# Latent attention as expanded 64-row heads, and differential before forgetting attention in one pipeline

## The reference

```python
# layer 2, even_mixer
o_a = fox_attention(aq, ak, av, log_f)     # 8 heads of 64; scores + (c_q - c_k), c = cumsum(log_f)
o_b = diff_attention(q1, q2, k1, k2, bv, lam)  # 4 heads, values of width 128; p1 - lam * p2
o_b = rms_norm_2(o_b, subln) * (1.0 - lam_init)
# layer 3, odd_mixer
c_kv = rms_norm_2(ckv, kv_norm)            # one latent of width 128 for all heads
q_abs = jnp.einsum('bshn,rhn->bshr', q_nope, w_uk)
o_lat = dsa_attention(q_abs, q_rope, c_kv, k_rope, iq, iw, ik, top_k)
    # s = (q_abs . c_kv + q_rope . k_rope) * scale over the selected keys; o = softmax(s) @ c_kv
o_c = jnp.einsum('bshr,rhd->bshd', o_lat, w_uv)
o_d = stick_breaking_attention(sq, sk, sv)
```

## Time and profile before

| what | value |
| --- | --- |
| median of 3 runs | 1994.19 us (1992.67 to 1994.88) |
| the profiled execution's own time | 1992.21 us |
| its span in the trace | 1990.4 us |
| PE busy | 1874.2 us, 94% |
| DVE busy | 1102.0 us, 55% |
| ACT busy | 758.8 us, 38% |
| POOL busy | 112.8 us, 6% |
| granted TensorE clock, mean | 0.971 of full |

### The profile page before, as it was taken

How to read it: one execution, slowest core, us unless ns; L and a number is a source line. 1 busy time by engine, 2 the same in 40 slices (tenths; PEclk the granted TensorE clock), 3 DMA queues, 4 the chain that set the end, 5 groups by cost and what they waited for, 6 DMA issues and landing times.

```text
span 1990.4 us, 23667 instructions
## 1 busy us (share of the span) xinstructions
PE 1874.2 (94%) x8984; PEld 1493.0 (75%) x8984; DVE 1102.0 (55%) x1661; ACT 758.8 (38%) x1094; POOL 112.8 (6%) x114
## 2 busy tenths in 40 slices
PE   4996999999999998779999999999978899999998
PEld 2884688888887887458888888877845688888886
DVE  4789554444323454664767663256895256767422
ACT  4225543333324212663544532232265344444321
POOL 0000010000011002601000000000000010000000
PEclk8997999999999998889999999998989999999999
DMA  4330032323232422002222232331200023223231
GB/s 149 128 106 22 7 111 94 105 84 105 85 111 101 149 85 85 1 1 84 88 103 99 91 106 92 118 101 60 91 16 1 22 85 106 92 98 105 85 106 64
DMA packets 25720, 166.26 MB, mean 84 GB/s; under 512 B 3082, under 2 KB 3210, under 8 KB 6704
## 3 DMA queue, kind: packets, MB, share of 16 engines
q1 hardware_dynamic: 23904, 159.88, 23.1%
q0 software_dynamic: 1744, 5.37, 0.9%
HBM read 163.10 MB, written 2.13 MB: 83 GB/s over the span
## 4 chain that ended last, share of the span: by engine, by line
PE 87%; DVE 6%; ACT 2%; POOL 2%; issue 1%; DMA 0%; SPq 0%; DVEq 0%; ACTq 0%
PE ps L365 25%; PE ps L367 25%; PE ps L366 25%; POOL tmp L331 2%; PE ps L538 2%; PE ps L380 2%; PE ps L379 2%; PE ps L378 2%; DVE cacc L1254 1%; PE ps L519 1%; PE ps L502 1%; DVE ring L1307 1%; PE ps L493 1%; PE ps L411 1%; ACT ring L877 1%
## 5 line engine op out<-in xcount | busy, mean ns | idle before, releaser
L365 PE MATMUL ps<-a_hi,w_hi 128*128 128x512 f32 x1616 | 636.9, 394 | 21.6 <-DVE w_lo L1079 16.6
L366 PE MATMUL ps<-a_lo,w_hi 128*128 128x512 f32 x1616 | 631.7, 391 | 0.0
L367 PE MATMUL ps<-a_hi,w_lo 128*128 128x512 f32 x1616 | 631.7, 391 | 0.0
L365 PEld LDWEIGHTS ps<-a_hi,w_hi 128*128 128x128 f32 x1616 | 305.3, 189 | 91.5 <-DVE w_lo L1079 17.8
L366 PEld LDWEIGHTS ps<-a_lo,w_hi 128*128 128x128 f32 x1616 | 305.0, 189 | 65.4 <-issue 2.4
L367 PEld LDWEIGHTS ps<-a_hi,w_lo 128*128 128x128 f32 x1616 | 304.9, 189 | 64.2
L1079 DVE TENSOR_TENSOR w_lo<-raw,w_hi 128x2048 fp32r<-128x2048 f32 x82 | 192.2, 2345 | 243.6 <-ACT w_hi L732 243.6
L732 ACT CAST w_hi<-raw 128x2048 fp32r<-128x2048 f32 x82 | 156.1, 1904 | 416.3 <-PE ps L367 337.8
L365 PE MATMUL ps<-h_hi,w_hi 128*128 128x512 f32 x528 | 206.3, 391 | 0.0
L367 PE MATMUL ps<-h_hi,w_lo 128*128 128x512 f32 x528 | 205.5, 389 | 0.0
L366 PE MATMUL ps<-h_lo,w_hi 128*128 128x512 f32 x528 | 205.5, 389 | 0.0
(11 more groups left out here) (215 smaller groups left out, 2061.3 us busy)
## 6 DMA issues: line engine op xcount, KB each, us to landing
raw<-weights_dram SPq DMA_DIRECT2D x148, 1024.0 KB, 4.8
xT<-x_in_dram SPq DMA_DIRECT2D x8, 256.0 KB, 7.4
bias_t<-bias_rows_scratch POOLq DMA_DIRECT2D x8, 256.0 KB, 5.0
ncb<-decay_rows_scratch POOLq DMA_DIRECT2D x8, 256.0 KB, 4.5
out_dram<-xT SPq DMA_DIRECT2D x8, 256.0 KB, 2.0
vec<-vectors_dram SPq DMA_DIRECT2D x1, 282.5 KB, 2.9
ring<-ramp_dram POOLq DMA_DIRECT2D x1, 260.0 KB, 5.2
tmp<-positions_dram POOLq DMA_DIRECT2D x1, 256.0 KB, 7.6
```

Of the source, the lines that this page charges most:

```text
L365: pe.matmul(dst, wh, hi[:, k0 + k, :], start=start and k == 0, stop=False)
L366: pe.matmul(dst, wh, lo[:, k0 + k, :], start=False, stop=False)
L367: last = pe.matmul(dst, wl, hi[:, k0 + k, :], start=False, stop=stop and k == nk - 1)
```

## The change

1. Latent heads: `ckv` is multiplied by `wuv` once per token block (`expand_values`, tile `v4`) and by `wuk` once per head pair (`expand_keys`, with the rotary key added on DVE), between slabs 5 to 9 of `in3`. `absorb`, `from_latent`, `ckv_t`, `olat` and the matmul L493 go. `dsa` units have one 64-row score matmul per lane and 64-column values into one bank, as `fox` has.
2. `diff` comes before `fox`, and both are one run of 32 units; the order of the value slabs of `in2` is changed to match. `fox` masks take `tmp` tiles 2 to 5, `diff`'s norm takes tiles 0 and 1 (in place), and `fg` moves from the ring to `tmp`.
3. `selm` is waited for by `dsa`'s first DVE step itself.

```diff
-KINDS = ((1, "moba"), (2, "fox"), (2, "diff"), (3, "sb"), (3, "dsa"))
+KINDS = ((1, "moba"), (2, "diff"), (2, "fox"), (3, "sb"), (3, "dsa"))
-        fg = ring2[0:HEADS, 4:7, :]
+        fg = tmp[0:HEADS, 1:4, :]
...
# POOL
-            for u in runs_of(2)[0]:
+            for u in runs_of(2)[1]:
...
-                a = (2 * u.m) % 4
+                a = 2 + (2 * u.m) % 4
...
# PE, scores
-                if u.kind == "dsa":
-                    for lane in range(2):
-                        pe.matmul(lane_scores(u, lane), qk3[:, 8 + 2 * u.p + lane, q], ckv[:, 0:u.w],
-                                  start=True, stop=False)
...
-                        qq, kk = qk3[f, 4 + u.p, q], qk3[f, 0, 0:u.w]
+                        qq, kk = qk3[f, 4 + u.p, q], qk3[f, KEYS[u.p], 0:u.w]
...
# PE, turn
+                    if u.kind == "fox" and u.m == 3 and lane:
+                        wait("df_ln", DIFFH)
...
+            def expand_values(t):
+                if t == 0:
+                    pe.wait_ge(sem["l3_in"], 32)
+                    wait("kv_dve", 2)
+                    wait("lg_relu", 12)
+                if t >= 2:
+                    wait("v_ev", t - 1)
+                pe.matmul(ps[:, 6 + t % 2, :], ckv[:, t * P:(t + 1) * P], wuv[:, :], start=True, stop=True
+                          ).then_inc(sem["v_mm"], 1)
+            def expand_keys(p):
+                if p < 2:
+                    wait("v_ev", p + 3)
+                else:
+                    wait("k_ev", p - 1)
+                pe.matmul(ps[:, 6 + p % 2, :], wuk[:, p, :], ckv[:, :], start=True, stop=True
+                          ).then_inc(sem["k_mm"], 1)
...
# PE, attend
-                    if kind == "diff" and 0 <= i - 3 < n and run[i - 3].last:
+                    if 0 <= i - 3 < n and run[i - 3].last and run[i - 3].kind == "diff":
                         h = run[i - 3].p
                         wait("df_sq", h + 1)
+                        if i < n and run[i].kind != "diff":
+                            wait("pt", 2 * run[i].n + 2)
...
-            for run in runs_of(2):
-                attend(run)
+            attend(UNITS[2])
...
-            for t in range(QT):
-                m = pe.transpose(ps[:, 6, t * P:(t + 1) * P], ckv[:, t * P:(t + 1) * P], ident)
-            m.then_inc(sem["kv_tr"], 1)
...
+            expand_values(0)
+            expand_values(1)
+            project("in3", 6)
+            expand_values(2)
+            expand_values(3)
+            project("in3", 7)
+            expand_keys(0)
+            expand_keys(1)
+            project("in3", 8)
+            expand_keys(2)
+            expand_keys(3)
+            project("in3", 9, tokens=True)
+            project("in3", 10, tokens=True)
...
+            wait("k_ev", 4)
             attend(runs_of(3)[0])
-            pe.wait_ge(sem["l3_in"], 32)
-            for p in range(4):
-                absorb(p)
-            wait("qa_ev", 4)
-            wait("qa_ev2", 4)
             attend(runs_of(3)[1])
...
# ACT, attend
+                    if 4 in norms:
+                        u = norms[4]
+                        wait("df_sum", u.p + 1)
+                        if u.p:
+                            wait("alo", LOWS["att2"] + u.p)
+                        A.activation(tmp[:, 1, :], ps[:, BT + 1, :], ACT.Ln, bias=col("eps"),
+                                     scale=1.0 / P).then_inc(sem["df_ln"], 1)
                     if 0 <= i < n:
                         move(run[i])
...
+                    if 4 in norms:
+                        u = norms[4]
+                        wait("df_ln", u.p + 1)
+                        A.activation(tmp[:, 1, :], tmp[:, 1, :], ACT.Exp, scale=-0.5).then_inc(sem["df_root"], 1)
...
+                if j in (5, 6):
+                    for t in (2 * j - 10, 2 * j - 9):
+                        wait("v_mm", t + 1)
+                        A.copy(v4[:, t, :], ps[:, 6 + t % 2, :]).then_inc(sem["v_ev"], 1)
...
# DVE
+                        wait("selm", u.qt + 1)
                         mask = selm[:, u.qt, 0:u.w]
...
+                if j in (7, 8):
+                    for p in (2 * j - 14, 2 * j - 13):
+                        wait("k_mm", p + 1)
+                        Vv.tensor_tensor(qk3[:, KEYS[p], :], ps[:, 6 + p % 2, :], qk3[:, 0, :], ALU.add
+                                         ).then_inc(sem["k_ev"], 1)
```

More of the change, by code:

```diff
@@ L237, in build @@
         BX, BT, BO = 3, 4, 6
+        KEYS = (1, 2, 3, 0)
         def lane_rows(lane):
@@ L501, in scores @@
                         qq, kk = QK[u.t][f, c + u.p, q], QK[u.t][f, c + 4 + u.p, 0:u.w]
-                    m = pe.matmul(lane_scores(u, lane), qq, kk, start=u.kind != "dsa", stop=u.kind != "sb")
+                    m = pe.matmul(lane_scores(u, lane), qq, kk, start=True, stop=u.kind != "sb")
                     if u.kind != "sb":
@@ L524, in values @@
                 if u.first and u.group >= 2:
-                    wait("oev", u.group if u.kind == "dsa" else u.group - 1)
+                    wait("oev", u.group - 1)
                 q = slice(u.qt * P, (u.qt + 1) * P)
@@ L915, in attend @@
                             exps(run[a])
+                    norms = {k: ends[i - k] for k in (2, 4, 6) if i - k in ends and ends[i - k].kind == "diff"}
+                    if 4 in norms:
[5 more added lines that the diff above has]
+                                     scale=1.0 / P).then_inc(sem["df_ln"], 1)
                     if 0 <= i < n:
                         move(run[i])
-                    if kind in ("moba", "fox", "sb") and i - 2 in ends:
+                    if i - 2 in ends and ends[i - 2].kind != "diff":
                         u = ends[i - 2]
@@ L944, in attend @@
-                    if kind == "dsa":
-                        if i - 1 in ends:
-                            u = ends[i - 1]
-                            wait("pv", u.n + 1)
-                            if u.p:
-                                wait("uv_mm", u.p)
-                            A.copy(olat[:, 0, :], ps[:, BO, :]).then_inc(sem["ol_ev"], 1)
-                        if i - 2 in ends:
-                            u = ends[i - 2]
-                            wait("uv_mm", u.p + 1)
-                            A.copy(a_hi[:, out_chunk(u), :], ps[:, BO, :]).then_inc(sem["ahi"], 1)
+                    if 2 in norms:
+                        u = norms[2]
+                        wait("pv", u.n + 1)
+                        if u.p:
+                            wait("df_sum", u.p)
+                        A.activation(tmp[:, 0, :], ps[:, BO + u.group % 2, :], ACT.Square
+                                     ).then_inc(sem["df_sq"], 1)
@@ L957, in _ @@
+                    if 4 in norms:
+                        u = norms[4]
+                        wait("df_ln", u.p + 1)
+                        A.activation(tmp[:, 1, :], tmp[:, 1, :], ACT.Exp, scale=-0.5).then_inc(sem["df_root"], 1)
+                    if 6 in norms:
+                        u = norms[6]
+                        wait("oev", u.group + 1)
+                        A.copy(a_hi[:, out_chunk(u), :], tmp[:, 1, :]).then_inc(sem["ahi"], 1)
             act.preload_act_table_set("natural_log_exp_and_others")
@@ L1301, in taken @@
                         wait("dec", u.m + 1)
-                        mask = tmp[:, (2 * u.m + lane) % 4, 0:u.w]
+                        mask = tmp[:, 2 + (2 * u.m + lane) % 4, 0:u.w]
                     elif u.kind == "diff":
@@ L1357, in attend @@
                         spare()
-                    if kind in ("moba", "fox", "sb") and i - 2 in ends:
+                    if i - 2 in ends and ends[i - 2].kind != "diff":
                         u = ends[i - 2]
                         fills[name] += 1
-                        c = (4 if kind == "sb" else 0) + u.p
+                        c = (4 if u.kind == "sb" else 0) + u.p
                         wait("ahi", FILL[name] + fills[name])
@@ L1608, in _ @@
                                  ALU.is_gt, ALU.mult).then_inc(sem["selm"], 1)
-            for p in range(4):
-                wait("qa_mm", 2 * p + 2)
-                Vv.tensor_copy(qk3[:, 9 + 2 * p, :], ps[:, 2 * (p % 2) + 1, :]).then_inc(sem["qa_ev2"], 1)
             attend(runs_of(3)[1])
```

86 lines of the change are left out of this document (17 added, 69 removed).

## The result

Four runs of the changed kernel have a median of 1963.54 us (1961.88 to 1963.57), four of the kernel before 1994.54 us (1992.67 to 1995.73) on the same chip: a ratio of 0.9843 [0.9826, 0.986]. The forecast was 1957 us, in a range of 1947 to 1968.

The account below looks back on a forecast made before the run. Bounds: POOL in layer 2's fox, PE in layer 3's dsa. Gains of 9.5 us (layer 2) and 27.4 (33.7 - 6.3, layer 3) sum to 36.9: 1957 us, inner band 1951 to 1963 (0.62), range 1947 to 1968.

Parts of the forecast that it names:

- the first rival: Layer 2 gives nothing, as the end of diff and the start of fox obstruct each other: 1967 us, chance 0.15.
- the three signs of being wrong: Mask gaps of more than 3 us, a dsa group above 11 us, or in3 slabs 6 to 9 late for an eviction.
- The run starts cold: Layer 2: diff starts where PE's granted clock was 0.50, without fox's cover; 1.5 us lost (0 to 3).
- the new wait: Layer 2, fourth fox unit: PE's second lane of turn waits for the last group's logarithm; 1.0 us charged (0 to 3).
- `out2` starts warm: End of layer 2: fox's short end precedes out2, so no cold start; 2.0 us given back (0 to 2).
- Layer 2's sum: Layer 2 in all: 10.0 - 1.5 - 1.0 + 2.0 = 9.5 us off.
- A latent group, 9.6 us: Layer 3, dsa: two round trips of 4.8 us, from scores to end of values, set each group; floor 8.8, ceiling 10.9.
- The rival of the engines' sum: Latent groups take 8.8 us through better overlap, start not slowed, new wait free: 1952, down to 1947; chance 0.13 under 1951.
- Start and end: Layer 3's latent run: 4.2 us from first take to fourth unit, 9.3 us from last take to last a_lo.
- `in3`: Layer 3: eight expansion matmuls add 6.9 us, four transposes go, evictions covered; 6.3 us net charged (to 8.3).
- 13 us groups: Layer 3: drains or banks keep a latent group near 13 us: 1967, at 15 us 1973; chance 0.07.
- a run slowed down by the clock throughout: PE is granted 0.50 in the latent run and in diff: 1999 us, slower than before; chance 0.03.

Follow-up runs that it names:

- the move first: The changed kernel with ACT's move of unit i ahead of its exponentials of unit i+3 in every attention run: 1947.62 us, ratio 0.9761.
- the three extra matmuls: The changed kernel with three unused 512-column matmuls on PE where it stands still at the start of the latent run: 1961.77 us, ratio 0.9837.
- doubling: The changed kernel with each of the eight expansion matmuls issued twice into the same place: 1970.48 us, ratio 0.9874.
- scores four ahead: The changed kernel with PE's scores issued four units ahead instead of three in every attention run: 1953.57 us, ratio 0.9795.

## Why the prediction was right

The sign, the range and the size of the largest terms held; the gain was put 5.9 us too high in medians (8.2 in spans). The 1963.5 us lie just above the inner band of 1951 to 1963, and it was the first rival that had stretched the range as far as 1968. Of the three signs of being wrong that the prediction names, one came: the masks show a gap of 5.46 us, where it allowed 3. So for layer 2 the account failed, though the number stayed in the range. Of the latent groups only the first is above 11 us, and no slab of `in3` began late. By the prediction's own steps:

**The run starts cold (1.5 us charged): wrong, little.** The clock was 0.50 from 788 to 796 us, but `diff` took 38.3 us from its first take to that of `fox`, the figure without the charge. The start took 4.4 instead of 4.2 us.

**`fox` behind it, 54.2 us plus 1.0 for the new wait: this is the term that was mis-sized.** From its first take at 824.16 to the end of the last `a_lo`, just ahead of `out2`, it took 62.8 us. Of the 8.6 us above 54.2, POOL's gaps are 6.9, where 1.0 was charged for the wait. The prediction followed one chain, from the logarithm to the tenth mask, and its elements are there: the logarithm behind `exps`, turn, values and scores, the take, the mask. It missed that the chain is entered late. The norm's matmul waits for the move of the third `fox` unit, a wait of the diff that the prediction's sum leaves out, and this move is behind the sixth unit's exponentials, whose take stands behind `diff`'s own `a_lo`. So the seventh unit was taken at 844.38, though its mask was there at 840.2. PE then ran the scores on the chain at the lower clock level: 1.62 and 2.08 us, against 0.92 and 1.13 at the upper one. The logarithm's place, with the clock that goes with it, is shown to carry 3.5 us. Mending the waits one by one didn't remove the gaps, and with the move first they went away entirely. Of the rest, 1.1 us is a longer emptying, in a stretch where the clock was at 0.54 to 0.61, and 0.5 lies in the masks themselves.

**`out2` starts warm (2.0 us given back): right.** 19 matmuls from 888 to 892 us against 11. At its start the changed kernel led by 0.5 us. At ACT's first cast of a slab behind it (900.07 us against 902.91) it led by 2.8, and still did at 1337 us.

**Layer 2's sum: 9.5 forecast, 1.3 within the run and 2.4 behind it.** The first rival, that layer 2 gives nothing, largely happened inside the attention run, by the mechanism that it names. With the move first, the merge gave 11.5 us, near the 10.0 that the prediction had read from the trace.

**A latent group, 9.6 us: 10.1, and 12.0 for the first.** The mechanism, a round trip that admits two units, was right, and two experiments show it: with scores admitted a unit earlier 8.6 to 8.8, with the move first 8.5 at a PE that never rests. The sums of busy time held too: in the group from 1512.73 us PE was busy for 8.79 us, DVE for 7.21 and ACT for 7.62, forecast 8.8, 7.3 and 7.7. Only the length of one of the two trips was off. From the 512-key unit's scores to those of the 256-key unit it is 4.73 us, which is the trip that the forecast read at 4.8; from there to the next 512-key unit's it is 5.38:

```profile
1510.74 1.13 PE L499 MATMUL ps<-qk 64*128 64x512 f32 x4
...
1515.47 0.70 PE L499 MATMUL ps<-qk 64*128 64x256 f32 x4
...
1516.38 0.69 DVE L1349 TENSOR_TENSOR a_lo<-ps,a_hi 128x512 fp32r<-128x512 f32 x1 [0.79 <-ACT a_hi L927]
1516.99 0.41 DVE L1293 CUSTOM_DVE_ANT_0 ring<-ps,selm 128x256 f32<-128x256 f32 x1
...
1520.85 1.13 PE L499 MATMUL ps<-qk 64*128 64x512 f32 x4
```

In the second trip the take of the 256-key unit (1516.99) comes 0.8 us after its scores are done: it stands behind the `a_lo` of the group before, which waits for ACT's `a_hi`. The forecast's trip has no group's end in it. This is read from the trace; no run moves that copy.

The first group's other 1.9 us are the clock, as the three extra matmuls showed: with the clock kept up this group takes 2.6 us less. The rival of the engines' sum named a floor that is real, but not what this order reaches.

**Start and end: right.** 3.5 us to the fourth unit (4.2 forecast), and 9.3 from the last take to the last `a_lo` (9.3).

**`in3`: right.** 6.5 us against 6.3; doubling cost 6.9 us. No slab began late for an eviction.

**Layer 3's sum:** 76.1 - 45.0 = 31.1 us from the masks to `out3`, and 31.1 - 6.5 = 24.6 us, against 27.4.

**Rest.** 1.3 us more were won between 1350 and 1362 us, where the clock was higher (0.87 from 1350 to 1355, 0.50 before), and 0.85 lost ahead of layer 2. Neither has work of the change in it. The first is luck: from the rotation at 1314.16 us to the one at 1361.56 the changed kernel took 47.4 us, and the kernel before 48.7. Of the twelve experiments, whose code is the same there, five took 47.5 to 47.6, one 48.2, and six, the move-first kernel among them, 48.6 to 48.8. With these the trace adds up: 1.3 + 2.4 + 1.3 + 24.6 - 0.85 = 28.7 us.

The rivals of 13 us groups and of a run slowed down by the clock throughout didn't come; the clock's price at the start of the latent run was 2.6 us, besides what it cost in layer 2.

**A better version than both** is the move-first kernel: 1947.62 us, 0.9761 [0.9748, 0.9774]. Of its 15.9 us against the kernel after, 11.2 are in layer 2 and 8.1 in the latent run; 1.2 go back between the last scan of the stick-breaking run and the first latent take, where the clock was 0.61 from 1484 to 1488 us. 1.4 go back between `out2` and the expansions, the same stretch that fell either way above. 0.8 are lost ahead of layer 2: layer 1's attention takes 1.4 us longer, with a clock of 0.82 and 0.50 from 208 to 216 us where it was 1.00. So the move first isn't free where a run empties. A move-first order for all but the stick-breaking run wasn't tried.

## What to carry to other kernels

On an engine that takes its work in order, the copy that frees a buffer should not stand behind work that waits for another engine: here the move stood behind exponentials that waited for DVE's take, and two swapped calls brought 16 us on top of the change's 31. In the kernel before they brought 6.6, and together with scores four ahead they made the kernel slower than either edit alone, so the swap has to be timed in each pipeline. When two pipelines are joined, write down for each wait of the one which step of the other it lands in, and at what time that step is reached, not only how long it takes; and count the emptying as work of the engines that do it, since it will collide with the next fill. A round trip read from a trace has to include what stands ahead of each step on its own engine, a group's closing copies above all.

## What was unexpected of the hardware

The granted clock fell from 1.00 to 0.51 at the start of the latent run after a stretch in which PE had been busy for 2.12 of 4 us, and for 2.85 in the stretch that ran low. With PE busy for 4.00 and 3.77 us there it didn't fall. In move-first the latent run was at 1.00 too, with PE at 2.59 and 2.88 of 4 us in its first two stretches. There the clock had fallen earlier, 0.61 from 1484 to 1488 us behind a stretch with PE busy for 2.30 of 4, and was back as the run began after 3.67 of 4. What decides between the two stays open. In the stall of layer 2 the lower level hit the chain itself: scores of 512 keys took 2.08 us there and 1.13 in the latent run at the upper one.
